# Copying the decay levels out before the weights' remainders, and moving forget gates and sample products to ScalarE, in the HGRN2 heads of a hybrid decoder step

## The reference, cut to what matters

```python
proj = h @ P['w_in_ab']
q_a, f_a, i_a, g_a, ... = split(proj)
lb = cumsum(softmax(hg_lb_logits))[layer]
log_f = log(lb + (1 - lb) * sigmoid(f_a))
k_a = (1 - lb) * sigmoid(-f_a)
# prompt, chunk by chunk; b = cumsum(log_f) in the chunk
dec = exp(where(causal, b[:, :, None] - b[:, None, :], -inf))
att = einsum('bthk,bshk,btshk->bhts', silu(q), k, dec)
o = att @ v + (silu(q) * exp(b)) @ s
s = exp(b_last)[..., None] * s + einsum('bshk,bshv->bhkv', k * exp(b_last - b), v)
# samples, one token: s = f * s0 + outer(k, v); o = s^T silu(q)
o_a = rmsnorm(o) * silu(g_a)
```

## Time and profile before

| | us |
|---|---|
| median of three executions (lowest, highest) | 2997.33 (2996.69, 3005.16) |
| the profiled execution, its own time | 3002.59 |
| its span in the profile | 3001.0 |
| busy PE, PEld, DVE, ACT | 2808.9, 2351.8, 1485.8, 1368.6 |
| HGRN heads, first VALUE pass to last norm | 497.9 to 843.3 |
| one turn of the loop (third head) | 591.4 to 633.1 |

### The profile page before, as it was taken

The page is one execution under the profiler, slowest core; times in us unless marked ns, Lnnn a source line. Parts: engine busy times, 40 slices in busy tenths (PEclk is TensorE's granted clock), DMA queues, the critical chain, the costliest instruction groups (busy, mean ns, idle before and its releaser), DMA issues.

```text
span 3001.0 us, 61100 instructions
## 1 busy us (share of the span) xinstructions
PE 2808.9 (94%) x24568; PEld 2351.8 (78%) x24568; DVE 1485.8 (50%) x2934; ACT 1368.6 (46%) x2100; POOL 44.7 (1%) x78
## 2 busy tenths in 40 slices
PE   6999997888889989999999999999989999999997
PEld 3899885777767868789988899888856667789996
DVE  1544327787858774544424544323336544544433
ACT  2434336555635444633435434344445545543443
POOL 0000000000010000000000000000000000000000
PEclk7999999898989999999999999999999999999998
DMA  6223442212212224222343223441346445322221
GB/s 243 85 93 111 167 162 75 84 65 78 86 68 74 89 101 189 78 99 91 123 183 123 71 98 112 167 156 66 135 155 186 150 147 200 113 85 89 98 97 67
DMA packets 58283, 349.37 MB, mean 116 GB/s; under 512 B 7537, under 2 KB 7874, under 8 KB 28578
## 3 DMA queue, kind: packets, MB, share of 16 engines
q1 hardware_dynamic: 52274, 322.85, 30.3%
q0 software_dynamic: 5872, 24.59, 2.3%
HBM read 334.96 MB, written 12.45 MB: 116 GB/s over the span
## 4 chain that ended last, share of the span: by engine, by line
PE 77%; ACT 8%; DVE 7%; issue 3%; DVEq 2%; DMA 2%; PEldq 0%; ACTq 0%; SPq 0%; POOL 0%; PEld 0%
PE PS L956 55%; PE PS L934 3%; PE PS L970 2%; PE PS L883 2%; PE PS L994 1%; PE PS L915 1%; PE PS L1414 1%; PE PS L890 1%; PE PS L978 1%; DMA weight_ring<-in_mla_pairs 1%; PE PS L1459 1%; PE PS L1349 1%; PE PS L1168 1%; ACT sub_out L1850 1%; ACT hgrn_w_hi L1644 1%
## 5 line engine op out<-in xcount | busy, mean ns | idle before, releaser
L2207 DVE TENSOR_TENSOR w_rest<-weight_ring,w_hi 128x1024 bf16<-128x1024 f32 (+1 forms) x268 | 320.8, 1197 | 856.9 <-ACT w_hi L1644 856.7
L1644 ACT ACTIVATE w_hi<-weight_ring 128x1024 fp32r<-128x1024 f32 (+1 forms) x284 | 294.8, 1038 | 889.0 <-PE PS L956 886.2
L956 PE MATMUL PS<-hid_hi,w_hi 128*128 128x260 f32 x2432 | 326.9, 286 | 0.0
L956 PEld LDWEIGHTS PS<-hid_hi,w_hi 128*128 128x128 f32 x2432 | 299.2, 188 | 2.3
L956 PE MATMUL PS<-hid_rest,w_bf 128*128 128x260 bf16 x2432 | 298.4, 274 | 0.0
L956 PE MATMUL PS<-hid_bf,w_rest 128*128 128x260 bf16 x2432 | 296.6, 274 | 0.0
L1645 ACT ACTIVATE w_bf<-weight_ring 128x1024 bf16<-128x1024 f32 (+1 forms) x284 | 289.6, 1020 | 0.0
L956 PEld LDWEIGHTS PS<-hid_bf,w_rest 128*128 128x128 bf16 x2432 | 235.6, 97 | 36.5
L956 PEld LDWEIGHTS PS<-hid_rest,w_bf 128*128 128x128 bf16 x2432 | 223.9, 97 | 38.6
L956 PE MATMUL PS<-gu_hi,w_hi 128*128 128x260 f32 x1232 | 168.7, 288 | 0.0
L956 PEld LDWEIGHTS PS<-gu_hi,w_hi 128*128 128x128 f32 x1232 | 152.8, 188 | 14.1 <-issue 11.2
(11 more groups left out here) (501 smaller groups left out, 4555.4 us busy)
## 6 DMA issues: line engine op xcount, KB each, us to landing
weight_ring<-in_ffn_gu SPq DMA_DIRECT2D x88, 1024.0 KB, 4.8
ada_chunks<-in_ada_w SPq DMA_DIRECT2D x40, 1536.0 KB, 6.6
weight_ring<-in_ffn_wd SPq DMA_DIRECT2D x32, 1408.0 KB, 6.1
weight_ring<-in_w_hgrn SPq DMA_DIRECT2D x16, 1024.0 KB, 4.9
weight_ring<-in_ada_w SPq DMA_DIRECT2D x8, 1536.0 KB, 8.0
weight_ring<-in_w_ssm SPq DMA_DIRECT2D x8, 1536.0 KB, 6.8
weight_ring<-in_mla_pairs SPq DMA_DIRECT2D x8, 1536.0 KB, 6.6
ada_chunks<-in_pages SPq DMA_DIRECT2D x40, 288.0 KB, 3.2
```

The source lines that it names most:

```text
L956: last = pe.matmul(PS[:, bank + hf, 0:HT], w[:, k * P:(k + 1) * P], x[:, first + k, hf * HT:(hf + 1) * HT], start=start and w is w_hi and ...
L1644: act.activation(hi, src, ACT.Copy).then_inc(w_hi_ready, 1)
L2207: tt(WL_[:, buf, 0:n], W[:, slot, j * DC * P:j * DC * P + n], WH[:, buf, 0:n].bitcast(F32), ALU.subtract).then_inc(w_rest_ready, 1)
```

## The change

- VectorE copies the levels out right after the levels' inputs. The samples' three parts come after them, then the attention block (`h_att`), and only then the remainders of the next head's FORGET and QUERY (in the last head: of the next stage).
- ScalarE copies the keys (`h_kdt`) after FORGET's weights and ahead of QUERY's.
- The outer products of the samples move from VectorE (two instructions of 128x512) to ScalarE: eight Identity activations of 128x128, with the key as a per-partition scale. VectorE makes state times gate plus product in one instruction per sample, eight in all.
- The forget gate's exponential, clamps and reciprocal are replaced by two Sigmoids at ScalarE, of f and of -f. VectorE keeps one instruction for the gate and one for the keys. The Sigmoid table is loaded ahead of the products; the Exp and Ln table after the two Sigmoids, ahead of the copies of VALUE's weights.

TensorE's program is the same, instruction for instruction.

```diff
--- before.py
+++ after.py
@@ -1824,15 +1824,24 @@
                 act.wait_ge(lb_exp, 1)
                 act.activation(LB, LB, ACT.Exp).then_inc(lb_exp, 1)
 
-                def forget_exp(h, ahead=0):
+                def forget_gates(h, ahead=0):
                     act.wait_ge(part_done, hgrn_group(h, FORGET) + (4 * ahead + 3))
-                    act.activation(two(E2), pair(2), ACT.Exp, scale=-1.0).then_inc(h_exp, 1)
+                    act.activation(two(E2), pair(2), ACT.Sigmoid)
+                    act.activation(two(E2R), pair(2), ACT.Sigmoid, scale=-1.0).then_inc(h_exp, 1)
+                    both_tables()
+
+                def sample_products(h):
+                    act.wait_ge(h_vb, h + 1)
+                    for b in range(NB):
+                        last = act.activation(VK[:, b, :], PS[:, 6 + b // 4, (b % 4) * P:(b % 4 + 1) * P],
+                                              ACT.Identity, scale=KK[:, NP_ + b:NP_ + b + 1])
+                    last.then_inc(h_vk, 1)
 
                 def forget_log(h, ahead=0):
                     act.wait_ge(h_f, h + (ahead + 1))
                     act.activation(EB, FG[:, 0:NP_], ACT.Ln).then_inc(h_lf, 1)
 
-                forget_exp(0)
+                forget_gates(0)
                 cut(0, VALUE)
                 forget_log(0)
 
@@ -1858,15 +1867,19 @@
                     act.activation(two(GS), pair(4), ACT.Silu).then_inc(h_exp, 1)
                     if more:
                         cut(h, FORGET, 1)
+                    else:
+                        ssm_cut(0, 0)
+                    act.wait_ge(h_kt, h + 1)
+                    act.activation(KDT.rearrange("p a b -> p (a b)"), PS[:, 4, :], ACT.Copy).then_inc(h_kdt, 1)
+                    if more:
                         cut(h, QUERY, 1)
                     else:
-                        ssm_cut(0, 0)
                         ssm_cut(0, 1)
-                    act.wait_ge(h_kt, h + 1)
-                    act.activation(KDT.rearrange("p a b -> p (a b)"), PS[:, 4, :], ACT.Copy).then_inc(h_kdt, 1)
-                    if more:
-                        both_tables()
-                        forget_exp(h, 1)
+                    if more:
+                        act.preload_act_table_set("sigmoid_and_others")
+                    sample_products(h)
+                    if more:
+                        forget_gates(h, 1)
                         cut(h, VALUE, 1)
                     act.wait_ge(h_o, h * 2 + 2)
                     act.activation(SQO[:, 0:NP_], PS[:, 6, :], ACT.Square)
@@ -2457,14 +2470,10 @@
                 def forget(h, ahead=0):
 
                     dve.tensor_copy(HP[:, 0:2], HVEC[:, 0:2, bass.ds(h + ahead, 1)].rearrange("p a b -> p (a b)"))
+                    dve.drain()
                     dve.wait_ge(h_exp, h * 3 + (3 * ahead + 1))
-                    ts(E2R, E2, 1e30, 1.0, ALU.min, ALU.add)
-                    ts(E2, E2, 1e30, None, ALU.min)
-                    dve.drain()
-                    dve.reciprocal(E2R, E2R)
-                    dve.drain()
-                    ts(FG, E2R, HP[:, 1:2], HP[:, 0:1], ALU.mult, ALU.add).then_inc(h_f, 1)
-                    stt(KK, E2, HP[:, 1:2], E2R, ALU.mult, ALU.mult)
+                    ts(FG, E2, HP[:, 1:2], HP[:, 0:1], ALU.mult, ALU.add).then_inc(h_f, 1)
+                    ts(KK, E2R, HP[:, 1:2], None, ALU.mult)
                     cut(h, VALUE, ahead)
                     dve.wait_ge(h_lf, h + (ahead + 1))
                     dve.tensor_tensor_scan(BB, const("reset"), EB, 0.0, ALU.mult, ALU.add)
@@ -2496,21 +2505,6 @@
                         k = KK[:, 0:NP_].rearrange("p (a c b) -> p a c b", c=2, b=m)
                         tt(d[:, :, 1, :], d[:, :, 1, :], q[:, :, 1, :], ALU.mult)
                         tt(d[:, :, 0, :], d[:, :, 0, :], k[:, :, 0, :], ALU.mult).then_inc(h_qk, 1)
-                    if more:
-                        cut(h, FORGET, 1)
-                        cut(h, QUERY, 1)
-                    else:
-                        ssm_cut(0, 0)
-                        ssm_cut(0, 1)
-                    dve.wait_ge(h_v, h + 1)
-                    tt(VR, VS, V3[0:NB], ALU.subtract)
-                    dve.drain()
-                    dve.tensor_copy(VM, VR)
-                    dve.drain()
-                    tt(V3[64:64 + NB], VR, VM, ALU.subtract)
-                    dve.tensor_copy(V3[32:32 + NB], VM)
-                    dve.drain().then_inc(h_vs, 1)
-
                     for n in range(1 + len(LEVELS)):
                         dve.wait_ge(h_p, h * 8 + (n + 1))
                         if n in (1, 2):
@@ -2528,18 +2522,30 @@
                             apart(dve)
                             dve.copy_predicated(AB, bcast(MSK[:, n - 1, :], 1, NCH), src).then_inc(h_ptk, 1)
                         dve.drain()
+                    dve.wait_ge(h_v, h + 1)
+                    tt(VR, VS, V3[0:NB], ALU.subtract)
+                    dve.drain()
+                    dve.tensor_copy(VM, VR)
+                    dve.drain()
+                    tt(V3[64:64 + NB], VR, VM, ALU.subtract)
+                    dve.tensor_copy(V3[32:32 + NB], VM)
+                    dve.drain().then_inc(h_vs, 1)
+
                     for at in range(0, CH, QR_):
                         dve.tensor_copy(AT[at:at + QR_, :, at:at + QR_], AB[at:at + QR_])
                     dve.drain().then_inc(h_att, 1)
+                    if more:
+                        cut(h, FORGET, 1)
+                        cut(h, QUERY, 1)
+                    else:
+                        ssm_cut(0, 0)
+                        ssm_cut(0, 1)
 
                     dve.wait_ge(s_loaded, h * 16 + 16)
-                    dve.wait_ge(h_vb, h + 1)
-                    tt(S0, S0, bcast(FG[:, NP_:T], 2, P), ALU.mult)
-                    for b in range(2):
-                        tt(VK[:, 4 * b:4 * b + 4, :], PS[:, 6 + b, :].rearrange("p (a b) -> p a b", a=4),
-                           bcast(KK[:, NP_ + 4 * b:NP_ + 4 * b + 4], 2, P), ALU.mult)
-                    dve.drain().then_inc(h_vk, 1)
-                    tt(S0, S0, VK, ALU.add).then_inc(s_new, 1)
+                    dve.wait_ge(h_vk, h + 1)
+                    for b in range(NB):
+                        last = stt(S0[:, b, :], S0[:, b, :], FG[:, NP_ + b:NP_ + b + 1], VK[:, b, :], ALU.mult, ALU.add)
+                    last.then_inc(s_new, 1)
 
                     dve.wait_ge(h_u, h + 1)
                     dve.wait_ge(s_stored, h + 1)
```

2 lines of the change are left out of this document (added).

## The result

The changed kernel takes 2969.11 us (median of 4 executions, 2959.3 to 2970.3), the kernel before 2997.01 us (4 executions, 2992.78 to 3005.16). The ratio is 0.9897 with a 95% interval of 0.988 to 0.9914: 1.0% faster, 26 to 36 us, at the mean 30.9. The forecast was 2966 us, by a sum of 31.6 us.

What follows compares the result with a forecast made beforehand. TensorE bounds the kernel, standing still mostly before the third level product. Gains of 5.0 + 6 x 3.6 + 5.0 = 31.6 us off 3002.6 give 2971.0, or 2965.7 from the median; predicted 2966, range 2956 to 2982.

Steps and rivals of the forecast that it cites:

- What bounds: TensorE's chain ends last; its largest hole, before the third level product, is 42.2 us in 8 heads.
- Levels, parts, `h_s`: Loop heads: levels move 5.3 us earlier, FORGET 5.0, `h_s` comes at 619.6, outputs start 3.6 us a head sooner.
- The keys' copy: ScalarE's copy of the keys, moved ahead of QUERY's weights: in time either way, costed at nothing.
- Products: Eight sample products at ScalarE take 2.3 to 2.9 us, done just when VectorE is free.
- Rival B: ScalarE's products end last at 4.7 us, costing 1.8 us a head; gain falls to 17.5, time 2980; 12%.
- The cover: ScalarE's products end barely before VectorE is free; every 0.1 us more for each costs 0.8 us a head.
- Sigmoids, `h_done`, ScalarE's chain: In the loop, earlier `h_done` gains nothing; TensorE waits 1.1 us instead of 0.5 for ScalarE's copy of the values.
- Table loads: At ScalarE each load costs 1.28 us, the next activation right behind; the skill's 2.7 us would make the sum 28.8.
- First head: Gains 5.0 us in all: 0.6 at the start despite a later first VALUE pass, and 4.4 more.
- Last head: 30 matmuls of 7.31 us replace FORGET and start 5.0 us sooner with L1179; 5.0 us gained.
- the three terms 5.0, 21.6 and 5.0: The sum's gains: first head 5.0 us, six loop heads at 3.6 us each, last head 5.0 us.
- Rival C: Slower: waits over 1 us before outputs and GATE's last pass make six projection passes run at low clock; 3033 us; 4%.

Runs made afterwards that it cites:

- levels first: The kernel before with only VectorE's levels, parts and attention block moved ahead of the two remainders; 2993.1 us, ratio 0.9974.
- three more table loads: The changed kernel with three needless activation table loads a head at ScalarE and the keys' copy back behind QUERY's weight copies; 2976.3 us, ratio 0.9907.
- products only: The kernel before with only the samples' outer products moved to ScalarE and eight combining instructions at VectorE; 3007.8 us, ratio 1.002.
- changed without products: The changed kernel with the samples' outer products back at VectorE in wide instructions, all else as changed; 2989.2 us, ratio 0.9965.
- the kernel laid out anew: The changed kernel with VectorE's parts between the levels' copies, prompt's states ahead of sample states, QUERY's remainder behind both; 2959.2 us, ratio 0.9859.

## Why the prediction was right

*What bounds.* Right: the 42.2 us in front of the third level were all TensorE's own time, and nearly all of them went (3.0 + 1.6 us are left).

*Levels, parts, `h_s`.* Right in every term within 0.4 us. From QUERY's end to the outputs it had 28.2 us (591.41 to 619.6) and the trace has 27.9 (574.2 to 602.1); the wait in front of L1191 was forecast as 1.4 us and is 1.52. The late remainder of QUERY moved it as counted. The 3.6 us a head are what the change gives against before's second trace (41.3 us a turn in the mean, 37.7 after). Against the first it is 4.2, and against the very head that the sum was worked out from 4.0; that the second trace gives just 3.6 is in part luck, since before's turns contain slow stretches that differ from trace to trace. The keys' copy was costed at nothing, and that was right, though not because it would have been in time: with the copy at its old place the states wait for it by 0.5 us (levels first, three more table loads), and in the latter kernel the outputs still wait the same 1.52 us for VectorE.

*Products.* Right: 2.18 us, hidden by 1.0 us in the loop. Rival B, with 4.7 us, is out. The cover was called thin, and with QUERY's remainder moved behind them it was gone (0.58 us of waiting). One sign that was named for a wrong prediction, a wait of VectorE for the products of more than 0.5 us, did show, in one place: 0.93 us in the first head of the first trace, where the states and L1179 ran at half pace; in the second trace it did not.

*Sigmoids, `h_done`, ScalarE's chain.* Right: alone they give 0.9998, and the wait for the values' copy went from 0.5 to 1.27 us (1.1 forecast). In the cover behind the Sigmoids, 2.6 us more cost 0.9 us a head (0.8 forecast).

*Table loads.* Each takes 1.28 us, and the next activation starts right behind it (601.78, 603.07). The 2.7 us of the Trainium skill (ScalarE: Activation LUTs, Rules for kernel authors) do not show here, and the measurement decides. The products cost ScalarE 2.18 us where VectorE had needed 1.28, yet at ScalarE they gave 20 us where VectorE was on the path, and lost 6 where it was not (products only: 0.2% of 3000). The rule of the same page and section that a multiplication belongs at VectorE therefore holds in the second case and not in the first.

*First head.* Undersized. From the stage's start to the transposes of the second head's values, the two traces of before took 63.5 and 61.4 us and the changed kernel's first trace 55.3: 8.2 and 6.1 us less, where 5.0 was forecast. VALUE's first pass started 5.13 us after the pass ahead of it, 3.35 us later than before, against 3.1 to 3.3 forecast. It ran at half pace (3.71 us), which the sum had not; in return GATE's last pass ran at full pace (1.95 instead of 3.38 us), which it had not either.

*Last head.* From the transposes of its values to the next stage the two traces of before took 32.8 and 30.8 us, those of the changed kernel 26.3 and 25.3. Against before's second trace that is 4.5 to 5.5 us, where 5.0 was forecast; against the first it is more. So the three terms 5.0, 21.6 and 5.0 came out, by before's second trace and the change's first, as 6.1, 21.7 and 4.5.

*Rival C.* The mechanism that was given 4% is real, and the change passed it by little. It needs not six slow passes: behind a wait of 3.1 us in front of the outputs 1.6 to 4.8 us were lost in eleven heads of two kernels, and nothing in one. The changed kernel waits 1.5 us there, and its loop has no slow pass. Had the products stayed at VectorE, the wait would have been 3.1 and 20 us of the gain would be gone. The argument against the rival, that FORGET's passes ran at full pace behind the 5.3 us, was read from one head and one row: the levels right behind that wait ran at 0.50, and FORGET's first pass took 2.62 us in the fifth head. The sum priced waits by their length; it could leave the clock out because the changed kernel's loop stays at full pace. Its other ground was that one long wait and two small ones become three of about 1 us. In the first head of the changed kernel's first trace a gap of 1.39 us in front of the states was followed by a clock of 0.50, so short gaps are no safeguard, and this part was in some measure luck. What the sum left out on the other side are before's own slow passes (its clock of 0.89 in the stage), which went too, and which differ from one trace of before to the next by 8 us.

What is still open: why the loss after the same wait of 3.1 us is 4.8, 3.2, 1.6 us or nothing in different heads, why short gaps lower the clock in some heads only, and why executions of one kernel differ by some 10 us outside the stage. No run looked into these.

## What to carry to other kernels

Work that an engine does for a later consumer (here the weights' remainders) should stand behind the work for which the busiest engine waits now; count what it is put in front of instead, since that sets the new end. Price a wait of TensorE not by its length alone: here a wait of 3.1 us cost 3 to 8 us with what followed it, so that idle matmuls in it, or a shortening to 1.5 us, gave more than the wait's length suggested. Take idle matmuls out again where the engine no longer waits. Measure such a change by several executions: one trace of each kernel gave 43 us, the medians 28 to 32.

## What the runs showed of the hardware

- Behind waits of 3.1 us TensorE went from 2.4 to 1.2 GHz (clock 0.50; L1197 3.41 instead of 1.84 us, a pass 3.81 instead of 2.16) in eleven of twelve heads (levels first, changed without products), with 1.6 to 4.8 us lost. With idle matmuls in the wait it did not fall behind the outputs in any head, nor behind waits of 1.5 us in front of the outputs (changed kernel).
- The length of the last wait does not decide it alone. The clock was 0.50 behind a gap of 1.39 us in front of L1175 (first head of the changed kernel's first trace) and 1.00 behind one of 1.12 us at the same place in the second trace; it was 0.59 behind a wait of 1.87 us (first head with three more table loads). Gaps of 0.41, 0.34 and 0.65 us between small matmuls were followed by a slow pass (2.63 us) in some heads of the kernel laid out anew and by full pace in others; with seven idle matmuls a head more it stayed at full pace in all loop turns.
- Eight 128x128 activations with a per-partition scale follow each other at 0.27 us (2.18 us for eight), and so do eight combining instructions of VectorE with a per-partition scalar, all of them in SBUF (2.19 us). This is near the 0.264 of the earlier trace rows, another VectorE instruction with a per-partition scalar, which reads PSUM.
- A load of an activation table took 1.28 us, and the next activation started right behind it. Of three more loads a head, the one in ScalarE's idle time left the outputs' wait at 1.52 us, and the two on its path made the turn 0.9 us longer.
